# Joined two-block kernel: hyena in two stages, attention with two sets of score banks, normed halves kept in DRAM, row fills issued inside the scan

## The reference

```python
# block 1: p = modulate(x, norm1_g, shift, scale) @ w_in, for lat and ctx; its columns feed
# pool mixer, attention, a bidirectional RWKV scan and the gates of their merge
def modulate(x, g, shift, scale):
    return rms_norm(x, g) * (1 + scale) + shift

# attention of block 1: 4 heads, two softmax maps each, keys of all 768 tokens
s = einsum('bqhmd,bkhmd->bhmqk', qb, keys) * DIFF_HEAD_DIM ** -0.5
p = softmax(s, axis=-1)
a = p[:, :, 0] - lam * p[:, :, 1]
return einsum('bhqk,bkhv->bqhv', a, vals)

# block 2, layer 0: hyena, for ctx (L = 256) and lat (L = 512) apart
g = v * x1
h = sin(fq * (z @ fw1 + fb1)); h = sin(fq * (h @ fw2 + fb2)); h = h @ fw3
h = h * (decay + HY_SHIFT)                       # hf, hb = its two halves
y = irfft(rfft(g, 2 * L) * rfft(k2))[:L]         # k2 from hf and the reversed hb
y = (y + g * bias) * x0

# block 2, layer 1: MLA attention, 8 heads of 128 + 64 wide keys, one softmax map
p = softmax(einsum('bqhd,bkhd->bhqk', q, k) * MLA_SCALE); einsum('bhqk,bkhd->bqhd', p, v)
```

## Time and profile before

| | |
|---|---|
| median of 3 runs | 4648.06 us (4647.92 to 4649.58) |
| the profiled execution | 4648.6 us |
| its span | 4646.4 us |
| mean granted clock of TensorE | 0.877 of full speed |
| instructions | 69318 |

### The profile page before, as it was taken

The page is one execution under the profiler, slowest core; times in us unless marked ns, Lnnn a source line. Parts: engine busy times, 40 slices in busy tenths (PEclk is TensorE's granted clock), DMA queues, the critical chain, the costliest instruction groups (busy, mean ns, idle before and its releaser), DMA issues. The chain is left out here.

```text
span 4646.4 us, 69318 instructions
## 1 busy us (share of the span) xinstructions
PE 3616.4 (78%) x29790; PEld 2818.8 (61%) x29790; DVE 1767.7 (38%) x3259; ACT 896.1 (19%) x1453; POOL 54.5 (1%) x70
## 2 busy tenths in 40 slices
PE   5879968568983777748778877899899578778887
PEld 3678947446653433326435757788788455656677
DVE  4645534651242000035324274544400543443333
ACT  2145512031111111121000241211100212222211
POOL 0000000000000000000000000000000000000000
PEclk7989978789985999978779988899999789977788
DMA  4130005103432999944211101344310010112222
GB/s 155 45 111 4 4 31 153 47 19 102 127 100 74 423 423 422 422 184 134 85 51 46 37 2 37 100 114 114 109 55 26 25 41 1 33 46 64 62 70 77
DMA packets 379842, 485.07 MB, mean 104 GB/s; under 512 B 16102, under 2 KB 325895, under 8 KB 371376
## 3 DMA queue, kind: packets, MB, share of 16 engines
q1 hardware_dynamic: 370592, 459.55, 28.4%
q0 software_dynamic: 3856, 13.11, 0.7%
q10 hardware_dynamic: 5120, 8.39, 0.5%
HBM read 455.84 MB, written 25.18 MB: 104 GB/s over the span
## 5 line engine op out<-in xcount | busy, mean ns | idle before, releaser
L288 PE MATMUL banks<-leading,w_rest 128*128 128x512 f32 (+2 forms) x1920 | 729.4, 380 | 121.4 <-DVE w_rest L248 121.4
L288 PE MATMUL banks<-rest,w_leading 128*128 128x512 f32 (+2 forms) x1920 | 717.5, 374 | 0.0
L288 PE MATMUL banks<-leading,w_leading 128*128 128x512 f32 (+2 forms) x1920 | 713.0, 371 | 0.0
L288 PEld LDWEIGHTS banks<-leading,w_rest 128*128 128x128 f32 (+1 forms) x1920 | 382.7, 199 | 195.2 <-issue 85.8
L288 PE MATMUL banks<-w_rest,leading 128*128 128x256 f32 (+3 forms) x1332 | 394.5, 296 | 65.1 <-DVE w_rest L248 65.1
L248 DVE TENSOR_TENSOR w_rest<-land,w_leading 128x1024 fp32r<-128x1024 f32 (+3 forms) x296 | 279.9, 987 | 393.4 <-ACT w_leading L242 393.4
L288 PEld LDWEIGHTS banks<-leading,w_leading 128*128 128x128 f32 (+1 forms) x1920 | 382.4, 199 | 64.4
L288 PEld LDWEIGHTS banks<-rest,w_leading 128*128 128x128 f32 (+1 forms) x1920 | 383.6, 200 | 60.0
L288 PE MATMUL banks<-w_leading,rest 128*128 128x256 f32 (+3 forms) x1332 | 390.3, 293 | 0.0
L288 PE MATMUL banks<-w_leading,leading 128*128 128x256 f32 (+3 forms) x1332 | 389.8, 293 | 0.0
L242 ACT CAST w_leading<-land 128x1024 fp32r<-128x1024 f32 (+3 forms) x296 | 239.0, 855 | 757.5 <-DMA land<-in_w_in 293.9
(11 more groups left out here) (529 smaller groups left out, 4860.6 us busy)
## 6 DMA issues: line engine op xcount, KB each, us to landing
wg<-in_w_exp_gate SPq DMA_DIRECT2D x32, 2048.0 KB, 28.4
wu<-in_w_exp_up SPq DMA_DIRECT2D x32, 2048.0 KB, 28.4
wd<-in_w_exp_down SPq DMA_DIRECT2D x32, 2048.0 KB, 27.9
ws<-in_ada_w SPq DMA_DIRECT2D x96, 512.0 KB, 3.9
land<-in_w_in SPq DMA_DIRECT2D x41, 1024.0 KB, 5.3
land<-in_ffn_up SPq DMA_DIRECT2D x44, 512.0 KB, 5.3
land<-in_ffn_up SPq DMA_DIRECT2D x88, 256.0 KB, 3.2
ws<-in_w_ada SPq DMA_DIRECT2D x32, 512.0 KB, 4.0
```

What stands on the lines that cost most here:

```text
L288: mm = nc.tensor.matmul(bank_of(r, kind, at), lhsT, rhs, start=(k == 0 and q == 0), stop=(k == kt - 1 and q == len(each) - 1))
```

## The change

Five edits:

1. **Row fills.** The three DMAs of zeros move from SP's program in `rwkv_start` to the start of SP's program in `rwkv_scan`. The memset of zeros stays where it was.
2. **Normed halves.** `normed_again` is gone. Beside the first projections POOL writes both halves of m.hT to a DRAM tensor (2 x 3.15 MB) and waits for them at the end of that stage. In `rwkv_result` POOL loads the leading half from its first stage on, the rest from its third, and waits for both at that one's end.
3. **Attention, maps = 2.** Score banks and `aT` are doubled; the scores of item i+2 are made while item i is worked on. One reduction serves both maps. `e` is no longer divided by its sum ahead of the transposes: one operation mixes both maps with the factor sum0 / sum1 x (-lam), and the division by sum0 comes with the last store.
4. **Attention, maps = 1.** `e` is transposed as it is; order on PE turns(i), scores(i+2), values(i); the pieces of a score row alternate between the 128-row and 64-row key parts.
5. **Hyena.** Two stages replace seven. The first holds the gate product, both layers for all 768 columns at once, all transposes (copied by ACT), the transforms of g (in the gaps of the sines and between filters) and the filters; the second the transforms of Kc and Ks with the products of spectra tile by tile beside them, and both inverse transforms. Tables for lat and ctx are loaded at the start; the inverse ones replace them.

SP ahead of the scan, before: the fills stand in rwkv_start.

The transforms of g now stand ahead of the filters, on both sides of the second layer. The core of the diff:

```diff
+            if pooled is not None:
+                @block.gpsimd
+                def _(pool):
+                    pooled(pool)
...
+                def scores(i, begun=True, ended=True):
+                    if i >= 2 and begun:
+                        pe.wait_ge(exped_sem, maps * (i - 1))
+                    pieces = [(q, c, w) for c, w in ((0, 512), (512, 256)) for q in range(maps)]
+                    for q, c, w in pieces:
+                        second = q > 0 and c > 0
+                        if not (ended if second else begun):
+                            continue
+                        k = c if q == 0 else 256 - c // 2
+                        if second:
+                            pe.wait_ge(begun_sem, i + 1)
                         parts = items[i][0][q]
                         for j, (lhsT, rhs) in enumerate(parts):
-                            for c, w in ((0, 512), (512, 256)):
-                                mm = nc.tensor.matmul(m.ps[:, 2 * q + c // 512, 0:w], lhsT, rhs[:, c:c + w],
-                                                      start=(j == 0), stop=(j == len(parts) - 1))
-                    mm.then_inc(scored_sem, 1)
+                            mm = nc.tensor.matmul(row(i, q)[:, k:k + w], lhsT, rhs[:, k:k + w], start=(j == 0), stop=(j == len(parts) - 1))
+                        if maps == 2 and q == 0 and c:
+                            mm.then_inc(begun_sem, 1)
+                    if ended:
...
+                scores(1)
+                if maps == 2:
+                    for i in range(n):
+                        if i + 2 < n:
+                            scores(i + 2, ended=False)
+                        if i:
+                            values(i - 1)
+                        if i + 2 < n:
+                            scores(i + 2, begun=False)
+                        pe.wait_ge(mixed_sem, i + 1)
+                        if i:
+                            pe.wait_ge(stored_sem, i)
+                        turns(i, b.a[:, i % 2, :])
+                    values(n - 1)
+                else:
+                    for i in range(n):
+                        pe.wait_ge(exped_sem, i + 1)
+                        if i >= 2:
+                            pe.wait_ge(stored_sem, i - 1)
+                        turns(i, b.e[:, i % 2, 0, :])
+                        if i + 2 < n:
+                            scores(i + 2)
+                        values(i)
...
+                def store(i):
+                    dve.wait_ge(valued_sem, i + 1)
+                    nc.vector.tensor_scalar(items[i][2], value_at(i), b.rec[:, i % 2, 0:1], None, ALU.mult).then_inc(stored_sem, 1)
...
+                    if maps == 2:
+                        if i:
+                            dve.wait_ge(mixed_sem, i)
+                        chain(nc.vector.tensor_scalar(b.mix[:, :], b.rec[:, i % 2, 1:2], b.sums[:, i % 2, 0:1], other_weight, ALU.mult, ALU.mult))
+                        if i >= 2:
+                            dve.wait_ge(turned_sem, i - 1)
+                        nc.vector.scalar_tensor_tensor(b.a[:, i % 2, :], b.e[:, i % 2, 1, :], b.mix[:, 0:1], b.e[:, i % 2, 0, :],
...
-        def normed_again():
-            with ExitStack() as rows:
-                m.x, m.xc = buffers(nc, rows, x=[NTL, D], xc=[NTC, D])
-                load(nc, [(m.x, a["x"].rearrange("(t p) d -> p t d", p=P)), (m.xc, a["ctx"].rearrange("(t p) d -> p t d", p=P))])
-                first_normed()
...
+        def keep(pool):
+            for part, x in enumerate(m.hT):
+                pool.dma_start(m.hT_dram[part], x[:, :, :]).then_inc(m.kept, 16)
+            pool.wait_ge(m.kept, 32)
+        products(nc, m, jobs, hT_of(m), evac, "vector", split=True, width=256, pooled=keep)
...
-            sp.wait_ge(done_sem, 1)
-            view = m.y_dram.rearrange("(p f) (h n) -> p (f h) n", p=P, n=512)
-            n = TAB * SLOTS // P // FILLS * (D // 512)
-            for f in range(FILLS):
-                sp.dma_start(view[:, f * n:(f + 1) * n, :], m.zeros[:, :].unsqueeze(1).to_broadcast([P, n, 512])).then_inc(m.filled, 16)
...
+            view = m.y_dram.rearrange("(p f) (h n) -> p (f h) n", p=P, n=512)
+            n = TAB * SLOTS // P // FILLS * (D // 512)
+            for f in range(FILLS):
+                sp.dma_start(view[:, f * n:(f + 1) * n, :], m.zeros[:, :].unsqueeze(1).to_broadcast([P, n, 512])).then_inc(m.filled, 16)
...
+            @block.gpsimd
+            def _(pool):
+                pool.dma_start(m.hT[0][:, :, :], m.hT_dram[0]).then_inc(m.back, 16)
...
+            @block.gpsimd
+            def _(pool):
+                pool.dma_start(m.hT[1][:, :, :], m.hT_dram[1]).then_inc(m.back, 16)
+                pool.wait_ge(m.back, 32)
...
+                    pe.wait_ge(landed_sem, 64)
+                    layer(b.w1, b.z, slice(0, 33))
+                    pe.wait_ge(gated_sem, 1)
+                    for t in range(NT):
+                        if t >= 2:
+                            pe.wait_ge(taken_sem, t - 1)
+                        for p in range(4):
+                            mm = nc.tensor.transpose(m.ps[:, 6 + t % 2, p * P:(p + 1) * P], m.hy[:, 4 + p, t * P:(t + 1) * P], m.ident)
+                        mm.then_inc(turned_sem, 1)
+                    pe.wait_ge(taken_sem, NT)
+                    for r in range(len(early) // 2):
+                        transform(r)
+                    pe.wait_ge(sined_sem, 1)
+                    layer(b.w2, b.h1, R)
+                    for r in range(len(early) // 2, len(early)):
+                        transform(r)
+                    pe.wait_ge(sined_sem, 2)
+                    pe.wait_ge(last_in_sem, 16)
+                    for t in range(NT):
+                        filters(t)
+                        if 1 <= t <= len(late):
+                            transform(len(early) + t - 1)
...
+                for r, (seg, table, f) in enumerate(order):
+                    if r >= 4:
+                        pe.wait_ge(read_sem, r - 3)
+                    dft(seg, table, f, (b.Kc, b.Ks)[table], r % 4).then_inc(made_sem, 1)
+                for seg in (1, 0):
+                    L, n = lengths[seg], counts[seg]
+                    pe.wait_ge(mixed_sem, n if seg else NT)
+                    if not seg:
+                        pe.wait_ge(read_sem, len(order))
+                    for p in range(4):
+                        for j, spec in enumerate((b.Gr, b.Ki)):
+                            if p == 0:
+                                pe.wait_ge(back_in_sem[2 * seg + j], 16)
+                            for f in range(n):
+                                mm = nc.tensor.matmul(m.ps[:, 4 * seg + p, 0:L], tiles_of(spec, seg)[:, f, p * P:(p + 1) * P], tables[seg][j][:, f, :],
+                                                      start=(j == 0 and f == 0), stop=(j == 1 and f == n - 1))
+                        mm.then_inc(out_sem, 1)
...
+                    dve.wait_ge(read_sem, 2 * i + 2)
+                    chain(v.tensor_tensor(b.t[:, :], gr, kr, ALU.mult))
+                    chain(v.tensor_tensor(kr, gs, kr, ALU.mult))
+                    chain(v.tensor_tensor(gs, gs, ki, ALU.mult))
+                    chain(v.tensor_tensor(ki, gr, ki, ALU.mult))
+                    chain(v.tensor_tensor(gr, b.t[:, :], gs, ALU.add))
+                    v.tensor_tensor(ki, ki, kr, ALU.subtract).then_inc(mixed_sem, 1)
```

More of the change, by code:

```diff
@@ L151, in bring_ahead, with products @@
     m.ahead_next += 1
-def products(nc, m, jobs, xT, evac, evac_on, banks=4, kt=KD, wslots=WSLOTS, beside=None, width=512, split=False, k_chunks=1, side=()):
+def products(nc, m, jobs, xT, evac, evac_on, banks=4, kt=KD, wslots=WSLOTS, beside=None, width=512, split=False, k_chunks=1, side=(), pooled=None):
     if split:
@@ L566, in attention @@
         b = Memory()
[L567 to L570, removed]
+        b.e, b.a, b.aT, b.mx, b.nb, b.sums, b.rec, b.mix = buffers(
+            nc, ctx, e=[2, maps, TOK], a=[2, TOK if maps == 2 else 1], aT=[2, TOK], mx=[2, maps], nb=[2, maps], sums=[2, maps], rec=[2, maps], mix=[1])
@@ new lines, in row, with rows, turned_at, value_at @@
+        def row(i, q):
+            first = (maps + 1) * (i % 2)
+            return m.ps[:, first:first + maps + 1, :].rearrange("p a b -> p (a b)")[:, q * TOK:(q + 1) * TOK]
+        def rows(i):
+            first = (maps + 1) * (i % 2)
+            return m.ps[:, first:first + maps + 1, :].rearrange("p a b -> p (a b)")[:, 0:maps * TOK].rearrange("p (q k) -> p q k", k=TOK)
+        def turned_at(i):
+            return 6 if maps == 2 else 4 + 2 * (i % 2)
+        def value_at(i):
+            return m.ps[:, turned_at(i) + 1, 256:256 + P]
@@ L571, in _ @@
+        with stage(nc, begun=1, scored=1, biased=1, exped=1, mixed=1, turned=1, copied=1, valued=1, stored=1, chain=1) as (
+                block, begun_sem, scored_sem, biased_sem, exped_sem, mixed_sem, turned_sem, copied_sem, valued_sem, stored_sem, chain_sem):
```

(22 more changed lines are left out.)

332 lines of the change are left out of this document (164 added, 168 removed).

## The result

The changed kernel takes 4461.06 us, median of 4 runs (4457.23 to 4465.53), against 4647.99 before: a ratio of 0.9598, 95% interval 0.9581 to 0.9614. Timed once more beside the kernel before on one chip it was 4452.9 against 4651.87, 0.9586 (0.9571 to 0.9601). The forecast was 4471 in a range of 4451 to 4500.

What follows compares the result with a forecast made beforehand. It took waits between engines and stage-end barriers as the bound, so savings add: fills -6.9, halves -44.6, attention -23.5, MLA -23.3, hyena -78.4, together -176.7 us from 4648.06, giving 4471 us, range 4451 to 4500.

## What to carry to other kernels

A DMA that rides "beside" landings that an engine waits for can hold them up until most of its bytes are out, with long rows and with short ones: put it where nothing lands (here 9 us for moving it, 0.6 at most for shorter rows). Where PE is the bound, the order of matmuls with different row counts is worth a look, since each pair of switches showed here as 0.39 us. Compare such long kernels stage by stage between barriers; the total has a scatter that hides edits of 5 to 10 us.

## What the runs showed of the hardware

Two queues with work shared the DMA engines' bytes in the ratio of their packets: about 24 to 1 with packets of 24 KB and 1 KB in the changed kernel, 3 to 1 with 3 KB and 1 KB. The first packet of a landing came 4.5 to 5.0 us after its issue beside such a write, 1.1 without. GpSimd's loads into fp32r, 3.15 MB each, landed after 10.9 and 10.2 us, no later than the plain load of 3.15 MB before (10 to 11 us). One switch between matmuls of 128 and of 64 rows cost 0.19 us. One long stage in which PE pauses again and again ran at a mean granted clock of 0.81 to 0.93 (374 to 340 us) in twelve profiles with no edit near it, and at 0.83 and 0.86 (367.8 and 359.1 us) in the same kernel.
